# Modulation weights read by output column and summed on VectorE, and a first stage in groups of two K blocks

## The reference, cut to what matters

```python
c_act = jax.nn.silu(c)                       # (1, 2048)
mod = c_act @ w_ada[l] + b_ada[l]            # (1, 12288)
sh_a, sc_a, gt_a, sh_f, sc_f, gt_f = split(mod, 6)
h = _rmsnorm(x, norm_mix[l]) * (1.0 + sc_a) + sh_a
p = h @ w_in[l]                              # c_q, c_kv, k_pe, q, k, v, z, b, a, gates
...                                          # attention, gated delta rule, their mix
x = x + gt_a * mix
h = _rmsnorm(x, norm_ffn[l]) * (1.0 + sc_f) + sh_f
gate, up = split(h @ w_gate_up[l], 2)
x = x + gt_f * ((silu(gate) * up) @ w_down[l])
```

## Time and profile before

| what | before |
|---|---|
| median of 3 executions | 2282.92 us (2281.2 to 2283.67) |
| the profiled execution | 2283.3 us |
| its span, first to last instruction | 2282.0 us |
| PE busy | 2227.7 us (98%) |
| DVE busy | 1514.7 us (66%) |
| ACT busy | 1017.8 us (45%) |
| moved by DMA | 507.81 MB, 223 GB/s over the span |

### The profile page before, as it was taken

How to read it: one execution, slowest core, us unless ns; L and a number is a source line. 1 busy time by engine, 2 the same in 40 slices (tenths; PEclk the granted TensorE clock), 3 DMA queues, 4 the chain that set the end, 5 groups by cost and what they waited for, 6 DMA issues and landing times.

```text
span 2282.0 us, 27023 instructions
## 1 busy us (share of the span) xinstructions
PE 2227.7 (98%) x10779; PEld 1856.2 (81%) x10779; DVE 1514.7 (66%) x1943; ACT 1017.8 (45%) x1287; POOL 24.5 (1%) x28
## 2 busy tenths in 40 slices
PE   5998999999999999999999999999999999999998
PEld 3778998888887888888888888887888888888886
DVE  5888998877759767765544555466556565655556
ACT  4345455333444464443344434456444444434444
POOL 0000000000000000000000000000000000000000
PEclk9999999999999999999999999999999999999999
DMA  9966868685778768865565565555565555555553
GB/s 361 381 242 203 276 222 276 197 281 185 238 283 292 282 233 285 275 236 197 188 198 185 185 203 185 190 197 194 187 201 189 189 189 189 189 186 195 198 189 132
DMA packets 278573, 507.81 MB, mean 223 GB/s; under 512 B 24104, under 2 KB 40240, under 8 KB 277424
## 3 DMA queue, kind: packets, MB, share of 16 engines
q1 hardware_dynamic: 278448, 506.09, 65.7%
HBM read 503.56 MB, written 2.50 MB: 222 GB/s over the span
## 4 chain that ended last, share of the span: by engine, by line
PE 81%; DVE 8%; DMA 4%; ACT 2%; issue 2%; SPq 1%; POOL 0%; DVEq 0%; ACTq 0%
PE bank L1212 24%; PE bank L1214 24%; PE bank L1213 24%; DVE WL L1954 3%; DMA RAW<-in_w_o_dram 2%; PE bank L1407 2%; ACT WH L1496 1%; DVE GA L1935 1%; PE bank L1133 1%; PE bank L1224 1%; PE bank L1226 1%; PE bank L1225 1%; DMA RAW<-in_w_in_dram 1%; DMA RAW<-in_w_o_gdn_dram 1%; PE bank L1160 1%
## 5 line engine op out<-in xcount | busy, mean ns | idle before, releaser
L1954 DVE TENSOR_TENSOR WL<-RAW,WH 128x1024 fp32r<-128x1024 f32 (+1 forms) x714 | 864.4, 1218 | 598.7 <-ACT WH L1496 596.9
L1496 ACT CAST WH<-RAW 128x1024 fp32r<-128x1024 f32 (+1 forms) x714 | 743.0, 1047 | 894.2 <-PE bank L1214 707.7
L1212 PE MATMUL bank<-WH,HTh 128*128 128x512 f32 x1936 | 766.0, 396 | 8.5 <-DVE WL L1954 8.0
L1214 PE MATMUL bank<-WH,HTl 128*128 128x512 f32 x1936 | 755.3, 390 | 0.0
L1213 PE MATMUL bank<-WL,HTh 128*128 128x512 f32 x1936 | 754.8, 390 | 0.0
L1212 PEld LDWEIGHTS bank<-WH,HTh 128*128 128x128 f32 x1936 | 364.3, 188 | 88.7 <-DVE WL L1954 13.2
L1214 PEld LDWEIGHTS bank<-WH,HTl 128*128 128x128 f32 x1936 | 364.0, 188 | 76.8
L1213 PEld LDWEIGHTS bank<-WL,HTh 128*128 128x128 f32 x1936 | 364.5, 188 | 74.8 <-issue 1.9
L1935 DVE SCALAR_TENSOR_TENSOR GA<-RAW,ST,GA 128x512 f32<-128x512 f32 x264 | 181.1, 745 | 12.4 <-DMA RAW<-in_w_ada_dram 7.7
L1212 PE MATMUL bank<-WH,R2h 128*128 128x512 f32 x408 | 162.0, 397 | 3.6 <-DVE WL L1954 3.6
L1213 PE MATMUL bank<-WL,R2h 128*128 128x512 f32 x408 | 159.9, 392 | 0.0
(11 more groups left out here) (280 smaller groups left out, 1773.0 us busy)
## 6 DMA issues: line engine op xcount, KB each, us to landing
RAW<-in_a_w_in_dram SPq DMA_DIRECT2D x96, 1024.0 KB, 5.1
RAW<-in_w_gate_up_dram SPq DMA_DIRECT2D x88, 1024.0 KB, 5.1
RAW<-in_w_ada_dram SPq DMA_DIRECT2D x80, 1024.0 KB, 5.3
RAW<-in_w_in_dram SPq DMA_DIRECT2D x63, 1024.0 KB, 5.0
RAW<-in_w_down_dram SPq DMA_DIRECT2D x44, 1024.0 KB, 5.0
RAW<-in_a_w_out_dram SPq DMA_DIRECT2D x32, 1024.0 KB, 5.0
A<-in_w_ada_dram SPq DMA_DIRECT2D x16, 1024.0 KB, 11.4
RAW<-in_w_o_dram SPq DMA_DIRECT2D x16, 1024.0 KB, 5.1
```

The lines of the kernel that those rows point to most:

```text
L1212: e.matmul(o, ah[:, s], hi[:, k, :], start=first, stop=False)
L1214: i = e.matmul(o, al[:, s], hi[:, k, :], start=False, stop=last)
L1496: e.copy(hi, rv).then_inc(S["hi"], 1)
L1954: e.tensor_tensor(lo, rv, hi.bitcast(F32), ALU.subtract).then_inc(S["lo"], 1)
```

## The change

The host hands the modulation matrix over transposed: 96 blocks of 1 MB, one for each 128 output columns, in which a partition holds one whole output column, 2048 values in a row. The biases, norm weights and convolution taps come as one array of columns instead of rows that PE transposed.

- `begin`: PE broadcasts the row `c` over all partitions with four matmuls of one row, ACT takes tanh, DVE writes 2 silu(c) to `CB` (128x2048, the same row on each partition).
- `ada`: one `tensor_tensor_reduce` for each unit multiplies it with `CB`, halves, sums along the row, starts from the bias and writes one column of `MOD`. The steps on ACT, the accumulators, and all matmuls and additions of the old way go.
- `front`: seven groups of two K blocks and two of one. The units of a group are 2n of `ada`, with the `ckv` and `conv` units of the group before between them, then `sm` and `cq` of this group. A unit of weights is split whole. Six places hold split halves in this stage instead of four. The low part of `h` is formed from a float32 copy that ACT writes too (it was DVE's L1995).
- Sum of squares and scaling of `x` are shared by ACT and DVE.
- `gate_store`, `gate_load`: the gates go as four columns of `MOD` to a row in DRAM (512 single values) and come back spread over the partitions, 512 values at a time, eight times each. Before, the bias rows were loaded in two transfers of 1 MB.

```diff
+GROUPS = [(2 * g, 2) for g in range(7)] + [(14, 1), (15, 1)]
...
     def plan_units(self, jobs, extra):
         u = self.units
-        u.extend(("g", ci, q) for ci in range(2) for q in range(4))
-        for c in range(4):
-            f = [("g", 2 * c + 2 + i // 4, i % 4) for i in range(8)] if c < 3 else []
-            w = [("w", j, 4 * c, 4) for j in jobs[:4]]
-            u.extend([w[0]] + f[:1] + [w[1]] + f[1:5] + [w[2]] + f[5:] + [w[3]])
+        sm, cq, ckv, conv = jobs[:4]
+        last = ()
+        for k0, n in GROUPS:
+            g = [("g", 16 + k0 + k) for k in range(n)] + [("g", k0 + k) for k in range(n)]
+            u.append(g[0])
+            if last:
+                u.append(("w", ckv) + last)
+            u.append(g[1])
+            if last:
+                u.append(("w", conv) + last)
+            u.extend(g[2:])
+            last = (k0, n)
+            u.extend([("w", sm) + last, ("w", cq) + last])
+        u.extend([("w", ckv) + last, ("w", conv) + last])
...
+            for n in range(4):
+                e.matmul(bank[n], ones[0:1, :], L.crow[:, 512 * n:512 * n + 512], start=True, stop=True).then_inc(S["c_t"], 1)
...
-            for t in range(2 if q == 0 else 0, 4):
-                g, col = L.GA[:, ci % 2, t % 2, :], L.cact[:, 4 * q + t:4 * q + t + 1]
...
-                e.scalar_tensor_tensor(out=g, in0=rv[:, t, :], scalar=col, in1=g, op0=ALU.mult, op1=ALU.add
-                                       ).then_inc(S["ga_dve"], 1)
...
+            e.tensor_tensor_reduce(out=rv, in0=rv, in1=L.CB, scale=0.5, scalar=COL[:, col:col + 1], op0=ALU.mult,
+                                   op1=ALU.add, accum_out=L.MOD[:, col:col + 1]).then_inc(S["ga_dve"], 1)
...
+        elif kind == "gate_store":
+            name, c = args
+            j = GATES[name] + 4 * c
+            W.wait_ge("ga_dve", sch.ga_of[j + 3])
+            dst = L.dram_gt[name == "gtf", 512 * c:512 * c + 512].rearrange("(j p) -> p j", p=P)
+            with L.nc.allow_non_contiguous_dma(reason="512 gate values"):
+                e.dma_start(dst, L.MOD[:, j:j + 4]).then_inc(S["gt_out"], 16)
+
+        elif kind == "gate_load":
+            name, c = args
+            n = c + 4 * (name == "gtf")
+            W.wait_ge("gt_out", 16 * n + 16)
+            W.wait_ge("gt_in", 16 * n)
             W.wait_ge("og_lo", 4)
             if name == "gtf":
                 W.wait_ge("to", 8)
-            j0 = 4096 if name == "gta" else 10240
-            e.dma_start(L.GT, spread_row(a["b_ada"][j0:j0 + D], D)).then_inc(S["bias_in"], 16)
+            cs = slice(512 * c, 512 * c + 512)
+            e.dma_start(L.GT[:, cs], spread_row(L.dram_gt[name == "gtf", cs], 512)).then_inc(S["gt_in"], 16)
```

More of the change, by code:

```diff
@@ L110, in make_jobs @@
              conv(0, O_Q)]
+    for j in front:
+        j.extra = EXTRA_R
     a1 = [conv(1, O_Q + 512), conv(2, O_K)]
@@ L393, in stage_next @@
         if u[0] == "g":
[L394 to L405, removed]
+            self.ada(i, u[1])
+            self.have |= {("mod", u[1] // 4)} if u[1] % 4 == 3 else set()
             self.issue_loads()
@@ L436, in fill, with ada @@
             self.stage_next()
[L438 to L453, removed]
+    def ada(self, i, col):
+        self.put("ada", i, col)
+        self.ga_n += 1
+        self.ga_of[col] = self.ga_n
+        self.marks[("raw_free", self.raw_slot(i))] = (("ga_dve", self.ga_n),)
+        self.staged[0] += 1
@@ L478, in front @@
[L478 to L503, removed]
@@ L504, in front @@
-        self.have |= {("mod", ci) for ci in range(8)} | {("ht", kt) for kt in range(16)}
-    def front_unit(self):
-        i = self.staged[0]
[L508 to L519, removed]
+        sm, cq, ckv, conv = jobs
@@ new lines, in front, with front_split @@
+        self.front_split(ckv)
+        self.front_split(conv)
+        self.put("load_cst2")
+        self.front_half(sm, 2)
+        self.front_half(cq, 0)
+        self.front_half(ckv, 1)
+        self.put("rope_tables")
+        self.front_half(conv, 3)
+        self.have |= {("ht", kt) for kt in range(16)}
+    def front_split(self, j):
+        i = self.staged[0]
+        _, uj, t0, nkt = self.units[i]
+        assert uj is j
+        hid = len(self.halves)
+        place = self.free_place(j)
+        self.place.append(place)
+        self.after.append(self.user[place] + 1)
+        self.user[place] = hid
+        self.halves.append((j, t0, nkt, i, 0, nkt))
+        self.put("split", hid)
+        self.marks[("raw_free", self.raw_slot(i))] = (("lo", hid + 1),)
@@ L520, in front_unit, with front_half @@
         self.staged[0] += 1
         self.issue_loads()
[L523 to L526, removed]
+    def front_half(self, j, where):
+        assert self.halves[self.used][0] is j
+        self.put("half", self.used, where)
+        self.used += 1
         j.end = self.used
@@ L894, in to_hl, with gate_rows @@
             yield
[L896 to L916, removed]
+    def gate_rows(self):
+        for name, j0 in GATES.items():
+            for c in range(4):
+                while ("mod", j0 // 4 + c) not in self.have:
+                    yield
+                yield
+                yield
+                self.put("gate_store", name, c)
+                for _ in range(3):
+                    yield
+                while (name, "free") not in self.have:
+                    yield
+                self.put("gate_load", name, c)
+                for _ in range(3):
+                    yield
+                self.have.add((name, c))
     def turn_chunk(self, n, c):
@@ L1923, in dve_program @@
+            e.tensor_scalar(COL[:, 96:192], COL[:, 96:192], 0.5, None, ALU.mult).then_inc(S["cols"], 1)
+            for n in range(4):
+                ns = slice(512 * n, 512 * n + 512)
+                W.wait_ge("c_th", n + 1)
+                e.scalar_tensor_tensor(out=L.CB[:, ns], in0=L.TH[:, ns], scalar=1.0, in1=bank[n], op0=ALU.add, op1=ALU.mult
+                                       ).then_inc(S["cact"], 1)
         elif kind == "ada":
-            i, ci, q = args
-            rv = L.raw(sch.raw_slot(i), 4, 512)
+            i, col = args
```

328 lines of the change are left out of this document (127 added, 201 removed).

## The result

The changed kernel takes 2292.51 us (median of 4, 2291.26 to 2297.30), the kernel before 2283.07: a ratio of 1.0047, interval 1.0029 to 1.0064. The change made it slower by about 9 us, where 18.5 us of gain were forecast. The profiled execution took 2291.26 us, its span is 2289.9.

A forecast was written before the change was run, and what follows sets the result against it. The first stage waits for weights, then PE and DVE are nearly full, and from 400 us PE bounds. -8.5 - 4 - 9 + 1.5 + 1.5 = -18.5 us gives about 2264 us, range 2246 to 2281.

The forecast's parts named there:

- Behind the first stage: From 155 us on: less work on DVE, ACT and PE gains 4 and 9 us, less 1.5 for clock, 1.5 for stores.
- I take 4 us of gain: From 155 to 400 us, with DVE and PE both near full: 4 us gained, bounds 0 and 7.
- I add 1.5 us in all: Eight gate stores of 512 single values: 1.5 us of cost in all, bounds 0 and 25.
- Rival 5: Gate stores hold up the weights, 4 us for six of them where ACT already waits for loads: 2289; 6 in 100.
- The weights behind a store are mostly loaded ahead: At the gate stores: the reason given for adding only 1.5 us in all.
- at most 6.2 us of the queue: Gate stores: queue time for 512 pieces, from 32 stores of 64 pieces each, one in 0.78 us.
- The row sum: The new 2048-column instruction on DVE: 2.45 us, bounds 2.3 and 2.6; the four steps it replaces took 2.74.
- Rival 3: The row sum on DVE runs at half rate, 4.6 us, ending at 2351 us, slower; 4 in 100.
- The first stage: Up to the seam: DVE's chain takes 137.7 us against 146.2, so the seam moves 8.5 us earlier, to 147.
- The clock: PE's pause before the next stage lowers its granted clock: 1.5 us added, bounds 0 and 4.
- Rival 4: PE's clock stays at half in the first stage, 18.8 us a group: 2295 us, slower; 5 in 100.
- the 9 us: From 400 to 1050 us, PE nearly always busy: 9 of 11.9 us of removed PE time come back; bounds 4 and 12.

The follow-up runs named there:

- g1: The changed kernel with one slot of waiting more ahead of the first attention step: 2279.00 us, 0.9987 of the kernel before.
- e1: The changed kernel with one slot of waiting less ahead of the first attention step: 2277.91 us, 0.9982 of the kernel before.
- e4: The kernel before with one slot of waiting more ahead of its first attention step, nothing else: 2299.12 us, ratio 1.0077.
- e3: The changed kernel with attention one slot earlier and no gate stores, gate rows loaded from the final norm's gain: 2261.17 us, 0.9909 of the kernel before.
- e2: The changed kernel without the eight gate stores, gate rows loaded from the final norm's gain: 2278.93 us, 0.9988 of the kernel before.
- f2: The changed kernel with attention one slot earlier and gate columns transposed on DVE, each row stored as 16 pieces of 128 bytes: 2260.90 us, 0.9907.
- f3: The changed kernel with attention one slot earlier and the 4-byte gate stores issued from ACT's queue instead of SP's: 2285.08 us, 1.0013.
- f1: The changed kernel with attention one slot earlier and each gate store writing 128 pieces of 16 bytes, read back with a stride: 2267.97 us, 0.9937.

## Why the prediction was wrong, step by step

**Missing: the slot.** "Behind the first stage" sums what DVE, ACT and PE lose and takes for granted that the order of the rest stays. It doesn't. When the kernel before came to the first part of a chunk and found its accumulator still in use, it stepped every background piece once more:

```diff
-            if q == 0 and self.ga_busy[ci % 2]:
-                self.forced = True
-                while self.ga_busy[ci % 2]:
-                    self.slot()
-                self.forced = False
```

The step list of before takes this loop twice, and the first time the step that falls into it is the attention's first. With the accumulators the loop goes, the attention starts one slot later, and since slots mostly alternate between a second-half split alone and a modulation unit with a first-half split, its steps change sides. That this loop is the origin is read from the code and from the list of steps that it writes, not from a run; that the slot costs 13.5 to 17.8 us is shown by g1, e1, e4 and e3. The step that failed is "I take 4 us of gain; the bounds are 0 ... and 7" for 155 to 400 us: up to 650 us the 11.2 us of the seam were lost and 0.9 more. The prediction had a row for it, DVE's 15 waits for ACT's copies, and read it as slack to be won, not as a wait that can grow. No rival spoke of it.

**Mis-sized: the stores.** "I add 1.5 us in all; bounds 0 and 25" measured 13.6 (e2) to 16.7 us (e3). Rival 5 had the mechanism and 25 us, with 6 in 100. The step that failed is "The weights behind a store are mostly loaded ahead": true from 850 to 1000 us, where PE is busy throughout (150.00 us) with stores in the queue, but not between 700 and 800, where three slots of `RAW` leave little lead and ACT already waited 36 us for `w_o`. The estimate of "at most 6.2 us of the queue" came from stores with pieces of 64 bytes; here one took 10.7 to land and held up what came behind it. The Trainium skill (DMA: Bandwidth & Descriptors, Specifications) says that below 512 bytes the DMA reads, modifies and writes. No run shows that step itself; pieces of 4 and 16 bytes were dear, while 16 pieces of 128 bytes (f2) cost nothing that can be measured here.

**The row sum, right.** 2.45 us were forecast with the read of the accumulator; a sum that follows another starts 2.27 us behind it (the sum's record is 2.345 long, the read's 0.08). Rival 3 is out: it wanted 4.6 us for two float32 sources from SBUF.

**The first stage, right and a little better.** Forecast -8.5, measured -11.2. The cheaper sums explain it: 32 times 0.18 is 5.8 us, of which a start some 0.7 us later (DVE's first sum, that of the squares, at 12.66 us where 12 was taken) and longer waits for ACT take part. DVE's last split was forecast for 137.7 and came at 135.0; the 9.2 us behind it were right (9.27).

**The clock, half right.** Rival 4 came in part: the granted clock was 0.89 over the first 142 us and 0.83 from 50 to 100, where PE was busy for 38.1 of 50 us (49.1 before, at 0.98). That PE's pauses in every group are the reason was not tested. It cost nothing there: PE was idle for 43 of the 142 us and then waited 5.81 us for DVE at the seam. The pause ahead of the next stage gave 0.74 from 142 to 155 us; what that costs (1.5 was added) can't be separated in these runs.

**The work behind the first stage, right once the two losses are out.** In f2, from PE's first matmul of the next stage (143.8, where the others have 144.2 to 144.9) to the first load of `w_o_gdn` it is 8.5 us shorter than before; then 2.0 longer up to `w_gate_up` (142.3 against 140.3, so nothing of the 9 us came in this stage), 4.3 shorter to the last load of `w_gate_up`, and equal to the end. That is -10.8, where -13 was taken. With the seam's 11.6 it makes 22.4 us of span. The forecast of 2264 was thus near what the change is worth (2261), not what it cost as it was made; and that nearness is in part luck, since 3.1 us more at the seam and the 3 us put in for clock and stores stand against 2.2 us less behind it.

## What to carry to other kernels

When a change takes out a wait that a scheduler or a step generator acts on, follow the order of the instructions in every later stage, not only where the change is: a slot's difference can cost more than the work removed (here 13.5 to 17.8 us). Of a stage in which two engines wait for each other in turn, ask what each has to do while the other is busy, and keep a piece of independent work behind each hand-over. Tiny pieces in a DMA are priced by what moves behind them; make rows on chip first (here 0.4 us of DVE for each row of 512).

## What the hardware showed that I had not expected

- A store of 2 KB in pieces of 4 bytes took 10.3 to 12.0 us to land (8 stores), and traffic fell from 381 to 142 GB/s for 7 us behind one of them. ACT's queue was no way round it. Behind 4-byte stores the times may also spread more: over 11 executions each, e1 ran from 2271.25 to 2282.03 us and e2, without stores, from 2277.42 to 2280.80; but f3, with stores, only from 2282.76 to 2287.33.
- With one operand read at a stride of four float32, a product of 128x512 takes 1065 ns where it took 686 (f1).
- With rows of 8 KB the saturated queue moved 403 GB/s from 50 to 100 us; with rows of 2 KB before, 380 GB/s in the same window. Other things differ there too, so the cause is not shown.
